# Moving loads, turns, group sums, token turns and cache copies in a two-layer hybrid decoder step on one core

## The chip, the core and the metric

The kernel runs on one core of a Trainium2 chip. A core has five instruction streams that run on their own and meet only at semaphores: TensorE (PE), VectorE (DVE), ScalarE (ACT), GpSimd (POOL) and SyncE (SP, here only a queue that issues transfers). Sixteen DMA engines move data between HBM and SBUF. The metric is the device time of one execution in microseconds (us), lower is better.

## The reference

One inference step of two decoder layers, for a prompt of 256 tokens and 8 decoding sequences of 4 tokens (288 token columns in all), D_MODEL 1024, everything in float32.

```python
def layer(h):
    p = rms_norm(h, norm_w) @ w_in            # q,k,v,gates, indexer, z, x/B/C, dt
    a = sparse_attend(top_k(indexer_scores))  # 4 heads; cache of 2048 rows in pages
    c = dilated_mix(q_c, k_c, v_c)            # 6 heads, windows 128/512/2048, dilation 1/4/16
    y = ssd_branch(z, xbc, dt)                # conv, chunked scan, gated group norm
    return h + concat(a*silu(g_a), c*silu(g_c), y) @ w_out
y = rms_norm(layer(layer(x)), final_norm_w)
```

The group norm divides `y` by the root of the mean square over each of two groups of 192 columns. The outputs are the two streams, the new key and value rows, the states, and the three window caches moved on by four rows; for the caches nearly all bytes are copied unchanged from an input in HBM to an output in HBM.

## The kernel before, in words

Activations lie transposed: 128 features on the partitions, 288 token columns in the free dimension, 8 tiles of features for D_MODEL. A layer is 35 input projection tiles (`proj0` to `proj34`) and 8 output tiles (`out0` to `out7`), each 8 products of a 128x128 weight block with 128x288 columns; the trace shows each product as two matmuls. Between the projections PE does the attention and state products, in an order written out by hand for each engine. Each use of a PSUM bank has a name and a fixed bank in `bank_plan`; `filled(use)` is counted up by PE, `drained(use)` by the engine that reads the bank, and the next use of the same bank waits for `drained` of the last one.

Weights come through four slots (`load_w`, SP queue): the slot of tile i is loaded again, for tile i+4, once tile i is done. Cache pages come through a ring of eight slots `kv`, even items issued by SP and odd ones by POOL, each when PE has used the item eight places earlier. POOL also issues `keep(layer, b, use)`: once `use` is filled, three transfers that copy the window caches of sequence b (2044, 508 and 124 KB) from HBM to HBM. There are 16 of these in all; `FRONT_KEEPS` are issued at the first projections of a layer, `STAGE_KEEPS` from `proj16` to `proj24`, `OUTPUT_KEEPS` behind the last ring item. POOL's last instruction waits for all of them (`copied`).

The stretches that the change touches, in PE's order:

- **Start.** SP loads x (8 tiles) in two transfers, `prm`, then the weights of `proj0`. DVE multiplies x by the norm weight (`weighted`), ACT squares it.
- **Mask and sparse exponential.** PE does two of the eight products of `proj28`, spreads the mask (`msk0` to `msk4`, when DVE's `mask_ready` is up) and does the other six. DVE adds the mask to the scores `srow` and takes the maximum; ACT does `sparse_exp(0..4)`; PE turns each exponentiated quarter (`pt0` to `pt3`); ACT evicts the turns (`sparse_turned`); PE does `value_groups`, 32 groups in all, in portions between the projections. POOL's products `y_gated` stand ahead of both.
- **Group sums and token turns.** ACT squares y (`ysq`); PE sums the squares over the partitions (`gn0`, `gn2`) after `proj30`, then `state_sums(1)`, then turns v of all tokens (`token_rows`: `vc0`, `vc1`, `va0` to `va2`), then `proj31`. DVE works through the last 8 of the `top8_round`s, `state_out(0..7)`, `prompt_mask(1)`, the inverse roots `inverse_group`, `group_normed`, and only then `dilated_scores(0)`.
- **Dilated attention.** `dilated_dots(0)` (PE) -> `dilated_scores(0)` (DVE) -> `dilated_exp(0)` (ACT, behind `evac(32)`) -> `dilated_probs(0)` (DVE) -> `dilated_turn(0)` (PE, after value group 17) -> `dilated_turned(0)` (ACT) -> `dilated_values(0)`; then the same for `qt` = 1.
- **Outputs.** `out0` to `out7`. DVE adds each to x, ACT squares the sum, DVE adds up squares (`add_square`), and PE sums them over the partitions with `sum_squares(L+1, 5)`, which stands between `out6` and `out7`.
- **End.** After the last root, DVE and POOL multiply by it: DVE the tiles 0 to 4 with one instruction each, POOL the tiles 5 to 7, which DVE had multiplied by the weight before. SP issues five transfers of y and waits for them. All engines then drain and meet.

## Time and profile before

| | |
|---|---|
| median of three runs | 609.94 us (609.93 to 610.36) |
| the profiled execution | 606.36 us |
| its span, first to last instruction | 604.6 us |
| busy in it: PE / DVE / POOL / ACT | 555.4 / 354.7 / 241.6 / 175.5 us |
| moved by DMA | 198.37 MB, mean 328 GB/s |
| granted TensorE clock, mean | 0.985 |

The profiled execution ran 1.76 us longer than its span. Idle time of PE is the span less its busy time, 49.2 us; where it lies, and what released PE after it, is what the rows further down are about. In this program the two layers are the same work at about 290 us distance, so a pattern of one stands for both unless said otherwise.

### The profile page before, as it was taken

What the parts mean: (1) busy time and instruction counts of PE and PEld (TensorE: products, weight loads), DVE (VectorE), ACT (ScalarE), POOL (GpSimd) and SP (SyncE); (2) the same over time, 40 slices, a digit from 0 to 9 for tenths busy, and PEclk for the clock granted to TensorE, in tenths of its full rate; (3) what the DMA queues carried; (4) which work ended last, traced back from release to release, by engine and by line L of the source; (5) the groups of instructions that cost most, each with busy time, mean ns of one, the idle gap of its engine ahead of it and who ended that gap; (6) DMA issues with size and microseconds to landing.
All of it is one profiled execution on the core that took longest, in us unless ns stands there. A gap on an engine that the chain in (4) does not pass through costs nothing.

```text
span 604.6 us, 13428 instructions
## 1 busy us (share of the span) xinstructions
PE 555.4 (92%) x4656; PEld 385.6 (64%) x4656; DVE 354.7 (59%) x1081; ACT 175.5 (29%) x457; POOL 241.6 (40%) x433
## 2 busy tenths in 40 slices
PE   4999999999999987999899999999999988799980
PEld 3776655677776654667677565557777755566760
DVE  4864655667776683534267563657678648553223
ACT  3013522112234342641001351311223344264110
POOL 0506642457327446261011474334843464631201
PEclk9999999999999997999999999999999999999996
DMA  8978999999999999798969999999999999993582
GB/s 328 318 279 296 369 368 386 414 355 354 397 395 348 335 307 359 245 347 295 376 208 370 296 362 372 374 417 360 368 367 379 383 336 315 345 322 98 201 302 78
DMA packets 75108, 198.37 MB, mean 328 GB/s; under 512 B 11585, under 2 KB 44770, under 8 KB 70946
## 3 DMA queue, kind: packets, MB, share of 16 engines
q1 hardware_dynamic: 53570, 99.50, 46.7%
q0 software_dynamic: 21472, 98.03, 44.1%
q8 instruction: 37, 0.61, 0.4%
q14 instruction: 29, 0.24, 0.1%
HBM read 189.33 MB, written 52.00 MB: 399 GB/s over the span
## 4 chain that ended last, share of the span: by engine, by line
PE 73%; DMA 9%; DVE 5%; SPq 5%; ACT 5%; issue 2%; DVEq 0%
PE bank L960 69%; DMA kv<-in_kk 6%; SPq L438 4%; PE bank L1006 3%; DMA w<-in_w 3%; ACT shared L765 1%; ACT srow L875 1%; ACT shared L748 1%; DVE shared L1838 1%; DVE shared L1821 1%; DVE st L1827 1%; DVE srow L2174 1%; SPq L434 0%; DVE xn L2256 0%; DVE shared L1785 0%
## 5 line engine op out<-in xcount | busy, mean ns | idle before, releaser
L960 PE MATMUL bank<-xn,w 128*128 128x288 f32 x1120 | 293.8, 416 | 8.2 <-DMA w<-in_w 8.2
L960 PEld LDWEIGHTS bank<-xn,w 128*128 128x128 f32 x1120 | 206.6, 191 | 77.0 <-issue 22.4
L438 POOL DMA_DIRECT2D kv<-in_kk x128 | 68.9, 539 | 91.4 <-PE bank L960 44.2
L438 POOL DMA_DIRECT2D kv<-in_vv x128 | 68.8, 539 | 90.5 <-PE bank L960 49.5
L701 ACT ACTIVATE pt<-bank 128x288 f32<-128x288 f32 x48 | 19.6, 409 | 191.9 <-PE bank L960 191.9
L960 PE MATMUL bank<-pt,w 128*128 128x288 f32 x256 | 64.1, 408 | 1.2 <-DMA w<-in_w 1.2
L960 PEld LDWEIGHTS bank<-pt,w 128*128 128x128 f32 x256 | 48.1, 190 | 15.4 <-DMA w<-in_w 2.0
L541 POOL DMA_DIRECT2D out_keep<-in_buf x48 | 25.0, 527 | 81.1 <-PE bank L960 79.3
L1696 DVE TENSOR_SCALAR_CACHE_REDUCE hit<-sc,tb 128x516 bf16<-128x516 f32 x62 | 46.5, 750 | 2.2
L960 PE MATMUL bank<-kv,qz 128*32 128x256 f32 x512 | 34.3, 385 | 0.0
L960 PE MATMUL bank<-kv,pt 128*32 128x256 f32 x512 | 33.5, 391 | 0.0
L2242 DVE TENSOR_TENSOR x<-x,bank 128x288 f32<-128x288 f32 x16 | 7.3, 454 | 40.0 <-PE bank L960 40.0
L1669 DVE COPY tails<-cin 128x3 f32<-128x3 f32 x14 | 4.8, 344 | 44.1 <-ACT cin L699 41.9
L960 PE MATMUL bank<-pt 64*128 64x128 f32 (+3 forms) x168 | 27.5, 351 | 0.0
L670 ACT ACTIVATE phased<-x 128x288 f32<-128x288 f32 x24 | 10.4, 442 | 58.5 <-DVE x L2242 52.7
L960 PEld LDWEIGHTS bank<-pt 64*128 64x128 f32 (+2 forms) x168 | 18.7, 193 | 11.6 <-issue 10.6
L1675 DVE SCALAR_TENSOR_TENSOR cacc<-cin,prm,cacc 128x312 f32<-128x312 f32 x42 | 22.8, 544 | 1.5
L1707 DVE TENSOR_SCALAR tb<-bank 128x1 int32<-128x1 f32 x62 | 9.6, 155 | 23.8 <-PE bank L960 23.1
L431 POOL DMA_DIRECT2D kv<-in_dil x16 | 8.7, 547 | 35.5 <-PE bank L960 35.3
L960 PEld LDWEIGHTS bank<-kv,pt 128*32 128x32 f32 x512 | 14.4, 111 | 12.1 <-issue 4.7
L960 PEld LDWEIGHTS bank<-kv,qz 128*32 128x32 f32 x512 | 13.4, 109 | 11.8 <-issue 6.3
L960 PE MATMUL bank<-kv,shared 128*32 128x128 f32 x576 | 18.6, 275 | 0.0
(262 smaller groups left out, 737.6 us busy)
## 6 DMA issues: line engine op xcount, KB each, us to landing
w<-in_w SPq DMA_DIRECT2D x86, 512.0 KB, 8.6
out_keep<-in_buf POOLq DMA_DIRECT2D x16, 2044.0 KB, 13.9
kv<-in_kk SPq DMA_DIRECT2D x128, 160.0 KB, 8.4
kv<-in_kk POOLq DMA_DIRECT2D x128, 160.0 KB, 5.8
kv<-in_vv SPq DMA_DIRECT2D x128, 128.0 KB, 4.8
kv<-in_vv POOLq DMA_DIRECT2D x128, 128.0 KB, 4.8
kv<-in_dil SPq DMA_DIRECT2D x16, 576.0 KB, 11.4
kv<-in_dil POOLq DMA_DIRECT2D x16, 576.0 KB, 8.1
```

Source lines behind the costliest of these rows:

```text
L431: engine.dma_start(kv[:, s, 0:9 * P], a["dil"][layer, item // NB * NB + SEQ_ORDER[item % NB]]).then_inc(S[f"kv_in{s}"], 16)
L438: engine.dma_start(kv[:, s, r * rec:(r + 1) * rec], a["kk" if what == "page" else "vv"][bass.ds(page + layer * N_POOL, 1)].rearrange("o p ...
L541: pool.dma_start(a[f"keep{g}"][bass.ds(layer, 1), b], a[f"buf{g}"][bass.ds(layer, 1), b, 4 * 256:], max_dma_last_dim=COPY_ROW).then_inc(S[ ...
L670: act.activation(squares[:, k % 2, 0:T], x[:, k, :], ACT.Square).then_inc(S["sq_ready"], 1)
L701: act.activation(ptile(i), src[:, 0:T], fn).then_inc(use, 1)
L748: act.activation(psa[:, i, 0:nk], psa[:, i, 0:nk], ACT.Exp, bias=st8[:, 1, i:i + 1], accum_out=st8[:, 2, i:i + 1]).then_inc(S["pexp"] if i ...
L960: return pe.matmul(out, lhsT, rhs, start=start, stop=stop, skip_group_check=True, **k)
L1006: return pe.transpose(out, in_, ident(n))
L1675: stt(out=o, in0=cin[:, n % 2, j:j + COUT], scalar=prmc(L, "cw", 4 * n + j), in1=o, op0=ALU.mult, op1=ALU.add).then_inc(S["cin_used"] if j ...
L1696: ts_(hit[:, :], sc[:, :], old.bitcast(F32), 0.0, ALU.is_ge, ALU.add, accum_out=cnt[:, 0:1]).then_inc(S["cnt_ready"], 1)
L1707: ts_(tb[:, 2:3], src[:, 0:1], float(TOPK_S), float(bit), ALU.is_lt, ALU.mult).then_inc(drained(f"count{n}"), 1)
L2242: tt_(x[:, m, :], x[:, m, :], src[:, 0:T], ALU.add).then_inc(drained(f"out{m}"), 1)
```

## The change

It reorders and moves; no arithmetic is removed.

- **Loads at the start.** x comes in four transfers of two tiles. SP issues `prm`, tiles 0-1, the weights of `proj0`, tiles 4-5; ACT issues tiles 2-3 and 6-7 as its first instructions.
- **Mask.** PE does one product of `proj28` ahead of the mask in place of two.
- **Turns.** ACT does the five `sparse_exp` in a row; DVE evicts `pt0` and `pt1` in place of ACT, and the `top8_round` that stood there moves behind.
- **Group sums.** ACT squares y ahead of `evac(28)`, loads the root's table with a small instruction, and takes the roots between `evac(29)` and `evac(30)`. PE does `gn0` between `state_sums(0)` and value group 6, `gn2` ahead of `proj30`. The banks of `gn2`, `ss4` to `ss7`, `vc1`, `va0` change.
- **Token turns.** From before `proj31` to after `proj32`.
- **Dilated exponential.** ACT does it ahead of `evac(32)`; DVE does `dilated_scores(0)` ahead of the second inverse and of `group_normed`, and `dilated_probs(0)` right after the second inverse.
- **Square sums.** `sum_squares(L+1, 5)` moves into `out7`, after five of its eight products.
- **Copies.** Each stage issues four in place of five; the second layer's end issues four in place of two, two of them at `proj34`. The front of layer 1 has two as before.
- **End.** DVE does all eight tiles, POOL none. SP issues two transfers of y, ACT two.

```diff
-FRONT_KEEPS = ((), ((0, 7, "proj1"), (1, 0, "proj4")))
-STAGE_KEEPS = (((0, 0), (0, 1), (0, 2), (0, 3), (0, 4)), ((1, 1), (1, 2), (1, 3), (1, 4), (1, 5)))
-OUTPUT_KEEPS = (((0, 5, "out0"), (0, 6, "out4")), ((1, 6, "out0"), (1, 7, "out2")))
+FRONT_KEEPS = ((), ((0, 6, "proj1"), (0, 7, "proj4")))
+STAGE_KEEPS = (((0, 0), (0, 1), (0, 2), (0, 3)), ((1, 0), (1, 1), (1, 2), (1, 3)))
+OUTPUT_KEEPS = (((0, 4, "out0"), (0, 5, "out4")), ((1, 4, "proj34"), (1, 5, "proj34"), (1, 6, "out0"), (1, 7, "out1")))
...
-                       ("gn0", 3), ("gn2", 2), ("ss4", 5), ("ss5", 6), ("ss6", 7), ("ss7", 3),
-                       ("vc0", 2), ("vc1", 5), ("va0", 2), ("va1", 6), ("va2", 5),
+                       ("gn0", 3), ("gn2", 3), ("ss4", 2), ("ss5", 5), ("ss6", 6), ("ss7", 7),
                        ("dot", 7), ("pd00a", 3), ("pd01a", 5), ("pd00b", 6), ("pd01b", 2),
+                       ("vc0", 2), ("vc1", 3), ("va0", 5), ("va1", 6), ("va2", 2),
...
-            for n in range(2):
-                sync.dma_start(x[:, 4 * n:4 * n + 4, :], a["x"][:, 4 * n:4 * n + 4, :]).then_inc(S[f"x_in{n}"], 16)
             sync.dma_start(prm[:, :, :], a["prm"]).then_inc(S["prm_in"], 16)
+            sync.dma_start(x[:, 0:2, :], a["x"][:, 0:2, :]).then_inc(S["x_in0"], 16)
             load_w(0, 0)
+            sync.dma_start(x[:, 4:6, :], a["x"][:, 4:6, :]).then_inc(S["x_in2"], 16)
...
-            for name, n, lo, hi in (("y_normed", 2, 0, 2), ("y_normed", 4, 2, 4), ("y_pooled", 2, 6, 8), ("y_normed", 5, 4, 5), ("y_pooled", 3, 5, 6)):
-                sync.wait_ge(S[name], n)
-                sync.dma_start(a["y"][:, lo:hi, :], xn[:, lo:hi, :]).then_inc(S["y_out"], 16)
-            sync.wait_ge(S["y_out"], 80)
+            for n in (0, 2):
+                sync.wait_ge(S["y_normed"], 2 * n + 2)
+                sync.dma_start(a["y"][:, 2 * n:2 * n + 2, :], xn[:, 2 * n:2 * n + 2, :]).then_inc(S["y_out"], 16)
+            sync.wait_ge(S["y_out"], 64)
...
                 feat(KC, KC + 3, 5)
-                keep(*STAGE_KEEPS[L][4], "proj24")
...
-            pool.wait_ge(S["rstd_ready"], nth(DEPTH, "rstd_ready", 1))
-            for k in (6, 7, 5):
-                pool.wait_ge(S["xw_ready"], nth(DEPTH, "xw_ready", k - 4))
-                pool.tensor_tensor(xn[:, k, :], xn[:, k, :], rstd[:, :], ALU.mult).then_inc(S["y_pooled"], 1)
...
         def _(act):
+            for n in (1, 3):
+                act.dma_start(x[:, 2 * n:2 * n + 2, :], a["x"][:, 2 * n:2 * n + 2, :]).then_inc(S[f"x_in{n}"], 16)
...
-                sparse_exp(0)
-                sparse_exp(1)
-                sparse_turned(0)
-                sparse_exp(2)
-                sparse_turned(1)
-                sparse_exp(3)
-                sparse_exp(4)
+                for c in range(5):
+                    sparse_exp(c)
                 sparse_turned(2)
                 sparse_turned(3)
...
-                evac(28)
-                evac(29)
-                evac(30)
                 for t in range(3):
                     act.wait_ge(S["y_ready"], nth(L, "y_ready", t + 1))
                     act.activation(xwf[:, t * T:(t + 1) * T], ptile(ZZ + t), ACT.Square).then_inc(S["ysq"], 1)
-                act.wait_ge(filled("gn2"), nth(L, "gn2"))
+                evac(28)
+                act.activation(warm[:, :], eps[:, :], ACT.Sqrt).then_inc(chain.next(), 1)
+                evac(29)
                 for t in (0, 2):
+                    act.wait_ge(filled(f"gn{t}"), nth(L, f"gn{t}"))
...
+                evac(30)
+                evac(31)
+                dilated_exp(0)
+                evac(32)
                 tokens("vc", 0, 256, 640)
                 tokens("vc", 1, 256, 640)
                 for tt in range(3):
                     tokens("va", tt, 0, 256)
-                evac(31)
-                evac(32)
-                dilated_exp(0)
                 dilated_turned(0)
...
-                proj(28, 0, 2)
+                proj(28, 0, 1)
                 pe.wait_ge(S["mask_ready"], nth(L, "mask_ready", 1))
...
-                proj(28, 2)
+                proj(28, 1)
...
                 proj(29)
...
                 state_sums(0)
+                group_sums(0, ((0, slice(0, P)), (1, half(0))))
                 value_groups(6, 9)
+                group_sums(2, ((1, half(1)), (2, slice(0, P))))
                 proj(30)
                 state_sums(1)
                 value_groups(9, 12)
-                pe.wait_ge(drained(f"y{2}"), nth(L, "y2"))
-                token_rows("vc", 0, VC, 3)
-                token_rows("vc", 1, VC, 3)
...
                 proj(32)
+                pe.wait_ge(drained(f"y{2}"), nth(L, "y2"))
+                token_rows("vc", 0, VC, 3)
+                token_rows("vc", 1, VC, 3)
...
-                for m in range(2, KT):
-                    output(m, (0, 1) if m == 2 else (5, 6, 7, 2, 3, 4, 0, 1))
-                    if m == KT - 2:
-                        pe.wait_ge(drained("pat11"), nth(L, "pat11"))
-                        sum_squares(L + 1, KT - 3)
+                output(2, (0, 1))
+                for m in range(3, KT - 1):
+                    output(m, (5, 6, 7, 2, 3, 4, 0, 1))
+                output(KT - 1, (5, 6, 7, 2, 3))
+                pe.wait_ge(drained("pat11"), nth(L, "pat11"))
+                sum_squares(L + 1, KT - 3)
+                output(KT - 1, (4, 0, 1))
...
-                top8_round(1)
+                dve.wait_ge(S["ki_out"], nth(L, "ki_out", 16))
+                dve.wait_ge(S["y_ready"], nth(L, "y_ready", 3))
+                for jg in range(2):
+                    dve.wait_ge(filled(f"pt{jg}"), nth(L, f"pt{jg}"))
+                    dve.tensor_copy(sct[:, 4 * jg:4 * jg + 4, :].rearrange("p j n -> p (j n)"), bank_of(f"pt{jg}")[:, :]).then_inc(drained(f"pt{jg}"), 1)
                 dve.wait_ge(S["sexp"], nth(L, "sexp", 5))
...
-                for n in range(4):
+                for n in range(6):
                     top8_round(1)
                 for b in range(4):
                     state_out(b)
                 prompt_state_out()
-                for n in range(3):
+                for n in range(2):
                     top8_round(1)
+                inverse_group(0)
                 for b in range(4, NB):
                     state_out(b)
                 prompt_mask(1)
-                inverse_group(0)
+                dilated_scores(0)
                 inverse_group(2)
+                dilated_probs(0)
                 group_normed()
-                dilated_scores(0)
...
-            for k in range(5):
+            for k in range(KT):
                 dve.scalar_tensor_tensor(out=xn[:, k, :], in0=x[:, k, :], scalar=fnw[:, k:k + 1], in1=rstd[:, :],
                                          op0=ALU.mult, op1=ALU.mult).then_inc(S["y_normed"], 1)
```

With it go the names of the semaphores (`x_in0` to `x_in3`; `y_pooled` is gone), the wait of each square and product of the start for its own quarter of x, and two y transfers at the end of ACT's program.

## Rows read from the trace of the kernel before

**Rows 1.** Waits of PE from 20 to 600 us: us in total, times, longest.

```profile
PE bank L1006 <- DVE shared L1838: 7.8, 4, 3.2
PE bank L1006 <- ACT srow L875: 3.9, 6, 0.7
...
PE bank L960 <- ACT xw L924: 3.0, 2, 1.5
PE bank L960 <- DVE phased L1622: 2.8, 2, 1.4
PE bank L960 <- ACT xw L927: 1.4, 2, 0.7
PE bank L960 <- DMA w<-in_w: 1.2, 1, 1.2
```

**Rows 2.** Timeline around the sparse exponential, layer 1: start us, us, instruction.

```profile
484.46 0.72 ACT L875 ACTIVATE srow<-srow,st 128x512 f32<-128x512 f32 x1 [1.86 <-DVE st L2182]
...
486.02 0.60 ACT L881 ACTIVATE pt<-bank 128x512 f32<-128x512 f32 x1
...
489.35 0.85 PE L960 MATMUL bank<-kv,pt 128*32 128x256 f32 x12
```

**Rows 3.** Groups by shape: count, busy us, mean ns, idle before.

```profile
L1918 DVE COPY sc<-bank 128x512 f32<-128x512 f32 x2 | 1.4, 690 | 5.6 <-PE bank L960 5.6
...
L1994 DVE TENSOR_TENSOR phased<-phased,bank 128x384 f32<-128x384 f32 x16 | 8.9, 554 | 0.6
...
L2009 DVE RECIPROCAL xw<-xw 128x288 f32<-128x288 f32 x4 | 7.8, 1953 | 0.1
...
L1733 DVE MAX8 top<-iacc 128x8 f32<-128x256 f32 x16 | 6.8, 428 | 0.6
...
L701 ACT ACT_TABLE_LOAD x8 | 10.3, 1283 | 0.1
```

**Rows 4.** Timeline of PE: dilated turns, layer 1's start, group sums.

```profile
235.68 1.54 PE L1006 MATMUL bank<-const,shared 128*128 128x128 f32 x6 [3.23 <-DVE shared L1838]
...
248.91 1.53 PE L1006 MATMUL bank<-const,shared 128*128 128x128 f32 x12 [0.58 <-DVE shared L1838]
...
301.81 4.04 PE L960 MATMUL bank<-xn,w 128*128 128x288 f32 x16
...
504.09 2.12 PE L960 MATMUL bank<-xw,ones 128*128 128x288 f32 x8 [1.49 <-ACT xw L924]
...
526.50 0.87 PE L1006 MATMUL bank<-const,shared 128*128 128x128 f32 x6 [3.23 <-DVE shared L1838]
...
537.19 1.53 PE L1006 MATMUL bank<-const,shared 128*128 128x128 f32 x12 [0.81 <-DVE shared L1838]
```

**Rows 5.** Windows: busy us of each engine, granted PE clock, DMA share, GB/s.

```profile
235.00:240.00 5.00, 4.32 (x26) 2.58 (x28) 0.63 (x2) 1.15 (x3) 2.15 (x4) 0.50 1.04 374
...
555.00:560.00 5.00, 4.58 (x25) 3.21 (x25) 2.81 (x4) 2.57 (x4) 0.00 (x0) 1.00 0.00 0
...
570.00:575.00 5.00, 5.00 (x22) 3.90 (x22) 0.95 (x3) 0.44 (x1) 0.00 (x0) 1.00 1.02 408
```

**Rows 6.** The chain that ended last, at the start: start us, us, what.

```profile
2.26 5.83 DMA w<-in_w
```

**Rows 7.** Weights issued at 286.57 us, copy issued at 568.35 us: us to landing.

```profile
w<-in_w SPq DMA_DIRECT2D x1, 512.0 KB, 14.5
...
out_keep<-in_buf POOLq DMA_DIRECT2D x1, 2044.0 KB, 20.0
```

**Rows 8.** GpSimd's last instructions: duration ns min/median/max, first and last start.

```profile
L226 POOLq DRAIN  x1: 10912/10912/10912, 593.5 to 593.5; - x1
```

**Rows 9.** VectorE's y products and GpSimd's, as in rows 8.

```profile
L2256 DVE SCALAR_TENSOR_TENSOR xn<-x,fnw,rstd x5: 503/1037/1046, 593.0 to 596.3; 128x288 f32<-128x288 f32 x5
...
L654 POOL TENSOR_TENSOR xn<-xn,rstd x3: 940/995/999, 593.2 to 595.1; 128x288 f32<-128x288 f32 x3
```

**Rows 10.** The y transfers, time from issue to landing.

```profile
DMA to landing us min/median/max: 2.1/2.3/2.5
```

More of the change, by code:

```diff
@@ L209 @@
 PER = {
-    "rstd_ready": 1, "sq_ready": 8, "sq_used": 5, "y_normed": 5, "y_pooled": 3, "z_gated": 1, "xw_ready": 8, "xn_free": 7, "xn_ready": 8, "roped": 15, "shuffled": 7, "ssum_ready": 1, "root_ready": 1,
+    "rstd_ready": 1, "sq_ready": 8, "sq_used": 5, "y_normed": 8, "z_gated": 1, "xw_ready": 8, "xn_free": 7, "xn_ready": 8, "roped": 15, "shuffled": 7, "ssum_ready": 1, "root_ready": 1,
     "qs_ready": 1, "relu_used": 1, "prelu_used": 8, "cnt_ready": NCOUNT + 1, "cin_used": 7, "tanhed": 7, "conved": 7,
@@ L331, in build @@
         S = {name: ctx.enter_context(nc.semaphore(name))
-             for name in ("x_in0", "x_in1", "ptab_in", "prm_in", "cst_in", "const_in", "ones_set", "zeroed", "act_chain", "dve_chain", "pool_chain", "y_out",
+             for name in (*[f"x_in{n}" for n in range(4)], "ptab_in", "prm_in", "cst_in", "const_in", "ones_set", "zeroed", "act_chain", "dve_chain", "pool_chain", "y_out",
                           *[f"w_in{n}" for n in range(WSLOTS)], *[f"kv_in{n}" for n in range(NKV)], *PER)}
@@ L664, in square @@
                 if N == 0:
-                    act.wait_ge(S[f"x_in{k // 4}"], 16)
+                    act.wait_ge(S[f"x_in{k // 2}"], 16)
                 else:
@@ L952, in _ @@
                 act.sem_clear(S["act_chain"])
+            for n in (1, 3):
+                act.wait_ge(S["y_normed"], 2 * n + 2)
+                act.dma_start(a["y"][:, 2 * n:2 * n + 2, :], xn[:, 2 * n:2 * n + 2, :]).then_inc(S["y_out"], 16)
         @block.tensor
@@ L1508, in _, with group_sums @@
                 proj(29)
-                state_sums(0)
-                value_groups(6, 9)
-                proj(30)
-                pe.wait_ge(S["ysq"], nth(L, "ysq", 3))
-                for t, parts in ((0, ((0, slice(0, P)), (1, half(0)))), (2, ((1, half(1)), (2, slice(0, P))))):
+                def group_sums(t, parts):
+                    pe.wait_ge(S["ysq"], nth(L, "ysq", 3))
                     pe.wait_ge(drained(f"gn{t}"), before(L, f"gn{t}"))
@@ L1518, in _ @@
                     ins.then_inc(filled(f"gn{t}"), 1)
+                state_sums(0)
+                group_sums(0, ((0, slice(0, P)), (1, half(0))))
+                value_groups(6, 9)
+                group_sums(2, ((1, half(1)), (2, slice(0, P))))
+                proj(30)
                 state_sums(1)
                 value_groups(9, 12)
-                pe.wait_ge(drained(f"y{2}"), nth(L, "y2"))
-                token_rows("vc", 0, VC, 3)
-                token_rows("vc", 1, VC, 3)
-                pe.wait_ge(drained(f"proj{VA + 1}"), nth(L, f"proj{VA + 1}"))
-                for tt in range(3):
-                    token_rows("va", tt, VA, 2)
                 proj(31)
@@ L1535, in _ @@
                 proj(32)
+                pe.wait_ge(drained(f"y{2}"), nth(L, "y2"))
+                token_rows("vc", 0, VC, 3)
+                token_rows("vc", 1, VC, 3)
+                pe.wait_ge(drained(f"proj{VA + 1}"), nth(L, f"proj{VA + 1}"))
+                for tt in range(3):
+                    token_rows("va", tt, VA, 2)
                 value_groups(16, 18)
@@ L1849, in _ @@
                     for k in range(KT):
-                        if k % 4 == 0:
-                            dve.wait_ge(S[f"x_in{k // 4}"], 16)
+                        if k % 2 == 0:
+                            dve.wait_ge(S[f"x_in{k // 2}"], 16)
                         weighted(0, k)
@@ L2212, in _ @@
                     tt_(gate, src[half(h2), 0:384].rearrange("p (g c n) -> p g c n", g=3, c=4)[:, :, :, h2:16:2], gate, ALU.mult).then_inc(drained("dot") if h2 else chain.next(), 1)
-                dilated_probs(0)
                 dilated_scores(1)
@@ L2245, in _ @@
                         weighted(L + 1, m)
-                    elif m >= 5:
-                        dve.wait_ge(drained(f"out{m}"), nth(L, f"out{m}"))
-                        ts_(xn[:, m, :], x[:, m, :], fnw[:, m:m + 1], None, ALU.mult).then_inc(S["xw_ready"], 1)
                     if 1 < m < KT - 1:
```

## The prediction

> **What bounds the kernel now.** I read the page first. PE is busy 555.4 of 604.6 us, and where the DMA engines work they are full, with a share of 1.02 to 1.04 [rows 5], so the question is who waits for whom. The waits of PE answer it [rows 1]: between 20 and 600 us PE waits for a weight transfer once, 1.2 us in all, and otherwise for VectorE and ScalarE in the stretch after the mask: 7.8 us for the dilated probabilities (four times, two of them 3.2 us), 3.9 for the sparse exponentials, 3.0 and 1.4 around the group sums, 2.8 for the square sums at a layer's end. PE's order sets the time, and what can be won is its idle time: these waits, the 8 us before its first matmul, and what lies behind its last. The timeline of PE [rows 4] shows where each wait lies; the windows [rows 5] show that the wait in layer 0 has a second price, a halved clock; the last rows [rows 8] show that the span ends with an instruction of GpSimd, not with the y transfers.
>
> **The start.** PE's first matmul follows the landing of `proj0`'s weights, issued at 2.26 us and 5.83 us on the way [rows 6]. Ahead of and with them went all of x, `prm` and the weights: 1152 + 51 + 512 = 1715 KB. Now tiles 4-5 (288 KB) are behind them; the tiles issued by ACT share the engines with them. At the 408 GB/s that a full window shows [rows 5], 288 KB are 0.7 us. If ACT's 576 KB took nothing from them, it would be 864 KB and 2.1 us; if the landing is set by something other than bytes, nothing. I take **-0.7**. DVE needs `prm` and tiles 0-1, which are now first; tiles 6-7 are wanted last.
>
> **Mask and exponentials, per layer.** PE spreads the mask right behind two products of `proj28`; the first exponential began at 484.46 and the value groups at 489.35 [rows 2]. One product is two matmuls, and a full window of 5 us holds 22 [rows 5]: 0.47 us sooner for mask, maxima and exponentials (nothing, if `mask_ready` is what comes last). The two evictions between the exponentials, 0.60 us each with 0.1 overlap, leave the chain: 486.02 was 1.56 behind 484.46 for two exponentials, so four now take 3.1 us, and 1.0 us is saved. DVE's copies of a 128x512 bank cost 0.69 each [rows 3]; they lie beside the third and fourth exponential, ahead of `px_ready`, which waits for the fifth anyway. If they did not hide, 0.7 of the 1.0 would be gone. PE waited 3.9/2 here in a layer, so 1.95 is the most. I take **-1.5**.
>
> **Group sums, per layer.** ScalarE squared behind `evac(30)`, and PE waited 1.5 us for the squares and 0.7 for the roots [rows 1, 4]. The squares now come ahead of `evac(28)`, two projections before PE wants them, and PE has three value groups or `proj30` to do while each root is taken: **-2.2**, at least 1.5 (the squares alone).
>
> **Dilated turns, per layer.** DVE did `inverse_group` twice (1.95 us each [rows 3]), `group_normed` and ScalarE `evac(32)` ahead of the first dilated softmax; PE waited 3.23 us for it in each layer [rows 4]. Now the scores come before the second inverse, which lies under the exponential; and the turns of v (1.5 us of PE) come after `proj32`, between scores and turn. The softmax is ready by my count 3 us before PE comes: **-3.2**. The second wait (0.6 and 0.8 us) stays, since the distance from `dilated_dots(1)` to it is what it was.
>
> **What is late next, per layer.** `dot` now takes bank 7 from `ss7`, which DVE drains last. DVE's queue from `state_sums(0)` on: `state_out(0..3)` 8 x 0.55 = 4.4, the prompt's state 2 x 0.55 = 1.1, two rounds of a MAX8 at 0.43, a replacement of the same size and small ones, 2.2, the first inverse 1.95, `state_out(4..7)` 4.4, together 14.1 us [rows 3]. PE does in that time the two group sums (8 matmuls, 2.0), `proj30` and `proj31` (16 each, 3.9), six value groups and `state_sums(1)` (64 small ones, 3.6): 13.4. PE waits **+0.7** for it (0 to 2: the sum of so many terms is no better). Behind it on PE stand the dilated dots. POOL's long wait for `ss7` only moves along. ScalarE gets one more table load in a layer, 1.28 us [rows 3], between two exponentials or while it waits for `proj32`: nothing, as the wait there is longer.
>
> The Trainium skill (ScalarE: Activation LUTs, What ACT_TABLE_LOAD costs) counts 2.66 us for a switch with its drain, where the row has 1.28. By that an eviction of v would be about 0.5 us late for `va2` in each layer, and the sum 1 us smaller.
>
> Per layer -1.5 - 2.2 - 3.2 + 0.7 = -6.2, for two **-12.4**.
>
> **The clock.** In layer 0 the wait of 3.23 us was followed by a window at a granted 0.50 [rows 5], that is 1.2 in place of 2.4 GHz. From the first dilated turn to the second PE took 248.91 - 235.68 = 13.2 us there, and 537.19 - 526.50 = 10.7 in layer 1, where the same wait left the clock alone [rows 4]. With the wait gone, **-2.5** (0 if another gap does it, the longest left there being 0.8 us).
>
> **Layer ends.** PE waited 1.4 us for the squares between `out6` and `out7` [rows 1]; five products (2.4 us) now cover it. In layer 1 that is -1.4. In layer 0 the weights of the next `proj0`, issued at 286.57, landed 14.5 us later, at 301.1 [rows 7], and that projection began at 301.8 [rows 4]. It can't begin before: **-0.7**, as the engines are full there.
>
> **Copies.** One copy (2044 + 508 + 124 KB) leaves each stage. No wait of PE in the stage was for a transfer, so I give nothing for it; it makes room for the same pages in less time. The end has four: two go out at `proj34`, when the engines stand idle (0 GB/s at 555 to 560 us [rows 5]). 5.35 MB at 408 GB/s are 13 us, which end before `out0` sends the other two and the last weights. The timeline has `proj34`'s end at 547 and `out0`'s at 565; no term of the sum comes from these two. They cost nothing there, and if they ran on past `out0`, the last copy would land later, which the end has room for (below).
>
> **The end.** DVE began y at 593.0. Of its five products those beside POOL's took 1037 ns, the one without 503 [rows 9]. PE's 1.4 us puts the start at 591.6; eight at 0.5 end at 595.6; ScalarE issues the last transfer, 2.5 us to land [rows 10]: 598.2. But the span ended with GpSimd's DRAIN, begun at 593.5 and 10.9 long, until 604.4 [rows 8], while the last product of y was begun at 596.3 [rows 9] and a transfer takes 2.5 [rows 10]. POOL's work now ends with the last copy, 568.35 + 20.0 = 588.4 [rows 7]. If the drain is 10.9 us long from there, it ends at 599.3; if it is 8.3 us behind POOL's last work (595.1 + 1.0 before [rows 9]), at 596.7. So the end lies between 598.2 and 599.5; I take 599.0, **-5.6** with layer 1's 1.4 in it.
>
> The rule against this part is in the Trainium skill (SBUF — State Buffer, Who interferes with whom): a VectorE instruction with two SBUF inputs and a GpSimd instruction that reads SBUF exclude each other. The trace agrees, 1037 against 503 ns, and it speaks for the change, since POOL has no product left. Without the rule eight products at 1.0 us would end at 599.9 and y land at 602.4, and the sum would be 3.4 us smaller.
>
> **Sum.** -0.7 - 12.4 - 2.5 - 0.7 - 5.6 = -21.9 us. On the profiled execution that is 606.36 - 21.9 = 584.5. The median of the runs shown is 3.6 us above it, which no row explains; I carry it along: 609.94 - 21.9 = **588.0 us**.
>
> **Rivals.**
> - *The drain does not move with POOL's work*, but ends as far behind everything as before. For it: the row shows one drain only, with nothing to compare. Then the end gives 1.4 in place of 5.6: 592.2 us. 15%.
> - *Transfers take the place of the waits.* A window in the stage has a DMA share of 1.04 at 374 GB/s [rows 5]: full. If the ring can't deliver in 6 us less, the stages return up to 12.4: 600.4 us, half of it 594.2. Against it: PE waited for no page there, and a copy of 2.7 MB less frees 7.2 us at that rate. 10%.
> - *The runs without a profile lose the clock in layer 1 as well*, which would explain most of the 3.6 us. Then 2.5 more come back: 585.5 us. 13%.
> - *The other side: the four copies end last.* POOL waits for them and drains after it. The rest is 16.3 us earlier, so the kernel is slower only if the last copy lands after about 610 on the old scale in place of 588.4, that is if the 10.7 MB of copies and 2.6 of weights from 549 on move at under 215 GB/s, where full windows show 374 and 408. At 200 GB/s: 614 us. 2%.
> - *It does nothing*, if each wait is replaced by the next one: 610 us. 2%.
> - The forecast, 583 to 592 by its own terms: 55%. The last 3% are losses that I don't see, between 595 and 609.
>
> The range from 583 to 595 takes in the clock rival, the drain rival and half the transfer rival. A change of 0.2%, 1.2 us, is about what a measurement of this kernel can tell from none. Faster by more 96%, within 1.5%, slower 2.5%.
>
> **What would show it.** PE's first matmul at 7.4 us; waits of PE for L1838 down from 7.8 to about 1.5 us, for the two ScalarE lines of the group sums gone, for the exponentials under 2; a new wait of 0.7 us for DVE's `state_out`, twice; no window at 0.50 inside; no wait between `out6` and `out7`; a DRAIN of POOL that begins at the last copy's landing and ends by 583 us. Wrong I would be with waits for `kv` or `w` in the stages, or a drain that still ends last by 4 us.

## The result

The changed kernel takes **586.82 us** (median of four runs, 584.74 to 590.63) against 609.93 for the kernel before (four runs): ratio 0.9636, 95% interval 0.9602 to 0.967, 23.1 us less. The forecast was 588.0 with a range of 583 to 595. The profiled execution took 584.74 us with a span of 583.1; the sum had put it at 584.5. It was the fastest of the four, 2.1 us under their median, where the kernel before had 3.6 us between the two.

The waits of PE from 15 us to the end (us in total, times, longest), to be held against [rows 1]:

```profile
PE bank L956 <- DMA kv<-in_vv: 4.5, 3, 2.1
PE bank L956 <- DMA kv<-in_kk: 2.9, 3, 1.1
PE bank L956 <- DMA w<-in_w: 1.3, 4, 0.5
PE bank L956 <- ACT relun L782: 1.1, 2, 0.6
PE bank L1002 <- DVE shared L1802: 0.8, 2, 0.4
PE bank L956 <- ACT phased L667: 0.5, 1, 0.5
PE bank L1002 <- ACT srow L872: 0.5, 2, 0.2
```

All the lines at which the change aimed are gone or small: the dilated probabilities (7.8 us), the two ScalarE lines of the group sums (3.0 and 1.4), the square sums (2.8); the exponentials are down from 3.9 to 0.5. In their place stand transfers: 4.5 us for value pages (`in_vv`), a line that the kernel before does not have, and four short waits for weights. [Rows 1] leave out this line of the kernel before:

```profile
PE bank L960 <- DMA kv<-in_kk: 3.4, 6, 0.9
```

These six waits for key pages, at 80 to 104 and at 370 to 395 us, lie ahead of the mask and are 2.9 us now.

The timeline of PE shows where the value pages are waited for. Start, duration, instruction, and in brackets the idle time before it:

```profile
195.95 3.11 PE L956 MATMUL bank<-kv,pt 128*32 128x256 f32 x48
...
227.79 0.87 PE L1002 MATMUL bank<-const,shared 128*128 128x128 f32 x6
228.59 1.07 PE L956 MATMUL bank<-kv,pt 128*32 128x256 f32 x16
229.59 1.57 PE L956 MATMUL bank<-pt 64*128 64x256 f32 x12
231.09 0.88 PE L956 MATMUL bank<-shared,vtok 128*64 128x128 f32 x12
234.05 1.08 PE L956 MATMUL bank<-kv,pt 128*32 128x256 f32 x8 [2.09 <-DMA kv<-in_vv]
235.06 5.28 PE L956 MATMUL bank<-xn,w 128*128 128x288 f32 x16
...
241.33 0.88 PE L1002 MATMUL bank<-const,shared 128*128 128x128 f32 x6
...
291.95 4.12 PE L956 MATMUL bank<-xn,w 128*128 128x288 f32 x16
...
509.03 0.87 PE L1002 MATMUL bank<-const,shared 128*128 128x128 f32 x6
...
515.22 0.64 PE L956 MATMUL bank<-kv,pt 128*32 128x256 f32 x8 [2.01 <-DMA kv<-in_vv]
...
520.92 1.53 PE L1002 MATMUL bank<-const,shared 128*128 128x128 f32 x12
```

The first dilated turn (227.79, 509.03) has no wait before it; one value group later, at group 20, PE stands still for 2.09 and 2.01 us until its page lands. `proj33` behind it takes 5.28 us in layer 0, where an undisturbed projection takes 4.15: part of it ran at half the clock. The windows (busy us of each engine, granted clock, DMA share, GB/s) say the same, and one thing more:

```profile
175.00:180.00 5.00, 5.00 (x43) 3.88 (x41) 3.99 (x14) 1.64 (x8) 0.00 (x0) 1.00 0.72 270
180.00:185.00 5.00, 5.00 (x86) 3.97 (x86) 2.43 (x9) 0.00 (x0) 1.47 (x3) 1.00 0.19 56
...
230.00:235.00 5.00, 2.91 (x32) 1.52 (x28) 3.96 (x8) 0.50 (x1) 3.72 (x8) 0.90 1.05 374
235.00:240.00 5.00, 5.00 (x20) 3.73 (x16) 1.84 (x5) 3.23 (x5) 0.48 (x1) 0.76 1.05 365
```

The clock of 235 to 240 us was 0.50 before [rows 5] and is 0.76 now. And the DMA engines, full from 190 to 245 us, are almost idle at 180 to 185, where the fifth copy of the stage used to be.

The end, in GpSimd's last instructions and VectorE's y products (ns min/median/max, first and last start; as [rows 8, 9]):

```profile
L226 POOLq COMPARE_BRANCH  x1: 41/41/41, 573.7 to 573.7; - x1
L226 POOLq DRAIN  x1: 8487/8487/8487, 573.9 to 573.9; - x1
...
L2259 DVE SCALAR_TENSOR_TENSOR xn<-x,fnw,rstd x8: 514/514/519, 577.0 to 580.0; 128x288 f32<-128x288 f32 x8
```

Eight products at 514 ns, no longer 1037, one every 0.43 us. The DRAIN is over at 582.38, the last y transfer lands at about 582.7, and the span ends at 583.1.

**Where the 21.5 us of span went.** From landmark to landmark on PE, change against the kernel before:

| stretch | forecast | measured |
|---|---|---|
| to the first matmul | -0.7 | -1.26 |
| to the value groups, layer 0; from the mask on, layer 1 | -1.5 each | -1.32, -1.18 |
| to the first dilated turn | -4.7 each | -5.31, -5.05 |
| to the second dilated turn | -2.5 (clock), 0 | +0.31, +1.20 |
| to `proj0` of layer 1 | -0.7 | -2.28 |
| to layer 1's mask (nothing edited) | 0 | -1.38 |
| to layer 1's last square sums | -1.4 | +0.21 |
| to the end | -4.2 | -5.44 |

### The profile page after: what moved, and what is told of

It reads as the page before. It is cut to its first block, busy times and chain, and to the rows that moved or that the text cites. A ratio compares the mean times of both kernels' runs of the same rounds, so it can differ in the third digit from the quotient of the medians.

```text
span 583.1 us, 13433 instructions
## 1 busy us (share of the span) xinstructions
PE 555.4 (95%) x4656; PEld 385.4 (66%) x4656; DVE 355.3 (61%) x1085; ACT 176.2 (30%) x457; POOL 238.7 (41%) x430
## 3 DMA queue, kind: packets, MB, share of 16 engines
q10 hardware_dynamic: 576, 1.18, 0.6%
## 4 chain that ended last, share of the span: by engine, by line
PE 73%; DMA 17%; SPq 3%; DVE 2%; issue 2%; ACT 2%; POOL 1%; POOLq 0%; DVEq 0%; ACTq 0%
PE bank L956 71%; DMA kv<-in_kk 7%; DMA kv<-in_vv 5%; DMA w<-in_w 5%; SPq L438 2%; PE bank L1002 2%; ACT shared L745 1%; DVE xn L2259 1%; DVE shared L1787 0%; DVE shared L1802 0%; DVE st L1792 0%; POOL kv L438 0%; DVE rstd L1615 0%; ACT pt L899 0%; SPq L434 0%
## 5 line engine op out<-in xcount | busy, mean ns | idle before, releaser
L698 ACT ACTIVATE pt<-bank 128x288 f32<-128x288 f32 x48 | 19.7, 410 | 180.3 <-PE bank L956 180.3
L956 PE MATMUL bank<-pt 64*128 64x128 f32 (+3 forms) x168 | 26.3, 334 | 0.0
L1709 DVE TENSOR_SCALAR tb<-bank 128x1 int32<-128x1 f32 x62 | 9.6, 155 | 23.8 <-PE bank L956 23.1
L956 PEld LDWEIGHTS bank<-kv,qz 128*32 128x32 f32 x512 | 13.4, 109 | 11.8 <-issue 6.3
## 6 DMA issues: line engine op xcount, KB each, us to landing
out_keep<-in_buf POOLq DMA_DIRECT2D x16, 2044.0 KB, 13.9
```

The source lines that it names most:

```text
L698: act.activation(ptile(i), src[:, 0:T], fn).then_inc(use, 1)
L956: return pe.matmul(out, lhsT, rhs, start=start, stop=stop, skip_group_check=True, **k)
L1709: ts_(tb[:, 2:3], src[:, 0:1], float(TOPK_S), float(bit), ALU.is_lt, ALU.mult).then_inc(drained(f"count{n}"), 1)
```

## The experiments

Each ran in rounds beside the kernel before on the same chip; the ratio is to that kernel. Its own median was 608.9, 609.4 and 608.0 us in the three sets (e1 to e4, e5 to e7, e8 to e10) over 11 to 15 runs. The sets ran on three chips, so experiments of different sets are compared by ratio: 0.001 is 0.6 us.

**e1, the start and the end alone**, on the kernel before: the diff's parts for the loads of x, the y products and the y transfers.

> The kernel before with two parts of the change alone: the loads at the start and the end (all eight y products on VectorE, two y transfers each from SP and ScalarE, none on GpSimd). Copies and everything between stay as before. Theory: the two parts are worth what the trace of the changed kernel shows at its two ends, first matmul at 6.9 us in place of 8.2 (-1.3) and 8.7 us in place of 14.0 from PE's last matmul to the end (-5.3): 609.9 - 6.6 = 603.3 us, GpSimd's DRAIN over before the y transfers land. Rival: the end's gain comes from the copies that land earlier in the changed kernel; here they land as before, GpSimd's DRAIN then ends last again, and the whole gives -1.3 to -3: 607 to 608.6 us.

Measured: 603.44 us, ratio 0.9898 (0.9864 to 0.9932). The first matmul started at 6.92 us, and PE's waits in between are those of before. The two ends are worth 5 to 6 us in the time, nearly what the theory said, without any help from the copies' new places. By landmarks they save 6.7 us (1.3 to the first matmul, 5.4 behind the last square sums), and 1.3 us in between are lost, where this profile has two windows at a clock of 0.66 in layer 1 that the kernel before does not have.

```profile
L226 POOLq DRAIN  x1: 8242/8242/8242, 589.9 to 589.9; - x1
```

The last copy landed at 589.6 here, the DRAIN behind it took 8.24 us and was over about 0.7 us before the y transfers.

**e2, the copies as before**, on the changed kernel:

```diff
-STAGE_KEEPS = (((0, 0), (0, 1), (0, 2), (0, 3)), ((1, 0), (1, 1), (1, 2), (1, 3)))
-OUTPUT_KEEPS = (((0, 4, "out0"), (0, 5, "out4")), ((1, 4, "proj34"), (1, 5, "proj34"), (1, 6, "out0"), (1, 7, "out1")))
+STAGE_KEEPS = (((0, 0), (0, 1), (0, 2), (0, 3), (0, 4)), ((1, 1), (1, 2), (1, 3), (1, 4), (1, 5)))
+OUTPUT_KEEPS = (((0, 5, "out0"), (0, 6, "out4")), ((1, 6, "out0"), (1, 7, "out2")))
+                keep(*STAGE_KEEPS[L][4], "proj24")
```

> The changed kernel with the copies placed as before: five in each stage (the fifth at proj24), two in each stretch of outputs. Theory: the engines are nearly idle at 180 to 185 us in the changed kernel (0.19), just where the fifth copy stood, and full from 190 on, so the copy is out of the way before the value pages are late. The waits of PE for value pages stay at about 2 us in each layer (4.1 to 4.9 us in all), the waits for weights in layer 1's outputs (1.3 us) go, and the time is 0.5 to 1.5 us under the changed kernel's 586.8: 585.3 to 586.3. Rival: the copy less is what paid for the pages that are now wanted sooner; then 2.7 MB more at 360 GB/s make PE's waits for pages grow by several us in each layer, and the time is 592 to 600 us.

Measured: 585.22 us (583.94 without its longest run), ratio 0.9598 (0.9538 to 0.9659), not to be told from the changed kernel. PE's waits for value pages are 5.3 us in place of 4.5, those for weights 2.4 in place of 1.3. The engines' share at 180 to 185 us is 0.96 again, no longer 0.19. So the rival is out: a copy more in the stage does not bring 592 to 600 us. But half of the theory is out as well: the weights of layer 1's last outputs come just in time here too. Two copies issued with them at `out0` to `out2` are enough for that; the two at `proj34` are not needed for it.

**e3, the late group behind the projection**, on the changed kernel:

```diff
-                value_groups(20, 21)
                 proj(33)
+                value_groups(20, 21)
```

(and SP's list of `next_w` follows: `(12, 18), (18, 20), (20, 26)`)

> The changed kernel with value group 20, the one that waited 2.1 us for its page in each layer, behind proj33 in place of ahead of it; nothing else moves. Theory: the page lands at its time whatever PE does, the engines being full up to it, and proj33 (4.1 us) covers it. The two waits of 2.0 us go; the second wait for the dilated softmax comes back (0.6 and 0.8 us before), and the window of layer 0 at half clock, which followed the wait (1.7 us of cost), goes or stays. So -2.6 without and -4.3 with the clock: 582.5 to 584.2 us. Rival: supply is behind by bytes, and the next groups (21 to 25) wait in its place: 586.3 to 587.3 us, with page waits of 4 us as before.

Measured: 581.4 us, ratio 0.9541 (0.9499 to 0.9583); again as e10: 582.27, 0.9574 (0.954 to 0.9608). From the first to the second dilated turn PE takes 10.68 us in layer 0 and 10.69 in layer 1, where the changed kernel takes 13.54 and 11.89. The waits at group 20 are gone, the second wait for the dilated softmax is back (1.6 us for both), and no window below full clock is left while PE works. The page itself is as late as before (issued from 221.3 us, landed at 234.7): `proj33` covers it. Of the rival, 0.87 us of waiting for a later page in layer 0 is left.

**e4, the dilated exponential's part undone**, on the changed kernel:

```diff
-                dilated_scores(0)
                 inverse_group(2)
-                dilated_probs(0)
                 group_normed()
+                dilated_scores(0)
+                dilated_probs(0)
...
-                dilated_exp(0)
                 evac(32)
+                dilated_exp(0)
```

> The changed kernel with the dilated exponential's part undone: VectorE does the scores behind the second inverse and group_normed, ScalarE the exponential behind evac(32). Theory: the pages set the floor of this stretch. PE waits 1 to 3 us for the first dilated turn again in each layer, but the wait for the page of value group 20 falls by the same, so that of up to 2 us in each layer nothing shows in the time: 586.8 to 589 us. Rival: the page wait is no floor but comes at its own place whatever precedes it (the order of the issues behind it sets it); then the waits add up, and the time is 589 to 593 us.

Measured: 589.22 us, ratio 0.9651 (0.9607 to 0.9694), by the medians 2 to 3 us over the changed kernel, where theory and rival meet; the intervals overlap, so the times do not decide. The waits of PE in the profile:

```profile
PE bank L1002 <- ACT vtok L738: 4.8, 2, 2.4
...
PE bank L956 <- DMA kv<-in_vv: 0.4, 1, 0.4
```

4.8 us of a new wait (ScalarE evicts the token turns only behind the exponential), and 4.1 us less for pages. In layer 0 the page landed at 233.7 us, 13.1 us after its issue, with the changed kernel at 234.0. The second dilated turn came at 240.95 us, with the changed kernel at 241.33: the page was the floor, and a first turn 2.5 us later cost nothing. In layer 1 the turn was late by 2.9 us counted from the mask, 1.5 us of it in a stretch at half clock. So in layer 0 the page took back what the dilated part of the change had gained; in layer 1 about half of it shows.

**e5, the changed kernel again.**

> The changed kernel once more, as the yardstick on this chip for the two beside it. Theory: 0.9636 of before again, and within a kernel the slower runs are those with the lower mean granted clock, since the windows at half clock come and go between runs. Rival: time and mean clock of the runs have nothing to do with each other.

Measured: 586.47 us, ratio 0.9613 (0.9572 to 0.9654). In this profile the page of group 20 cost 3.80 us in layer 0 and 2.14 in layer 1. Time and clock go together, but not closely: the kernel before took 604.6 us at a mean granted clock of 0.988 and 612.2 at 0.981 (the ends of ten of its eleven runs), the changed one 584.87 at 0.996 and 590.65 at 0.988 (of six). In e10 the fastest and the slowest of five runs, 5.0 us apart, had 0.994 and 0.995, so part of the spread is not the clock's.

**e6, layer 1's last copies late, SP waits for them**, on the changed kernel: `(1, 6, "out4"), (1, 7, "out5")`, and `wait_ge(S["copied"], ...)` moved from GpSimd's end to SP's.

> The changed kernel with two edits at its end: the last two copies of layer 1 go out at out4 and out5 in place of out0 and out1, and SP in place of GpSimd waits for all copies. Theory: in layer 1 the weights of out4 to out7 landed 5.7 to 13.2 us after their issue because two copies stood on the engines with them; without those they land in 5 to 8 us, PE's waits for weights in layer 1's outputs (about 1.3 us, with the weight loads' own 2.6) go, and PE ends 1.5 to 2.5 us sooner. GpSimd's DRAIN, 8.2 to 8.5 us long wherever it begins, now begins near 560 us and ends by 570; the last copy (20 us from issue at 560 at most) lands before y: 584.5 to 585.5 us. Rival: the weights queue behind what was issued earlier (the copies of proj34), and nothing changes; or the last copy ends last: 587 to 590 us.

Measured: 585.84 us, ratio 0.962 (0.9572 to 0.9668): no difference that shows. At PE the theory holds: no output of layer 1 waits for weights, and it gets from the turn ahead of the outputs (544.65 us in the changed kernel) to the last square sums in 27.1 us, the changed kernel in 28.9. The end gives it back:

```profile
L226 POOLq DRAIN  x1: 19153/19153/19153, 562.8 to 562.8; - x1
...
L226 SPq DRAIN  x1: 7/7/7, 580.8 to 580.8; - x1
```

The DRAIN begins at 562.8 as wanted and lasts 19.15 us, until 581.97: 4.3 us behind the last copy's landing at 577.7. The theory had it 8.2 to 8.5 us long wherever it begins; that step is refuted.

**e7, the copies spread**, on e3: two at the front of layer 0 (`proj4`, `proj6`), five in each stage, one at `proj34` in each layer, none in the outputs.

> Value group 20 behind proj33 as in e3, and the copies where the trace of the changed kernel has room: two in the front of layer 0 (proj4, proj6), the fifth one back at proj24 in each stage (the engines were at a share of 0.19 there), one at proj34 in each layer and none in the outputs; SP waits for all copies. Theory: e3's 581.4, less the weight waits of both layers' outputs (3 us at PE in e3: 1.5 in each layer) and of the first projection of layer 1: 577.5 to 580 us, page waits of the stages as in e3. Rival: copies in the front of layer 0 delay its weights or first pages, and give back what the outputs gain: 581 to 583 us.

Measured: 593.52 us, ratio 0.9729 (0.9683 to 0.9775), 12 us over e3. By ratio it is 9 to 11 us. The rival had the direction; its size was some four times too small. The timeline of PE:

```profile
52.05 7.08 PE L957 MATMUL bank<-xn,w 128*128 128x288 f32 x16 [5.56 <-DMA w<-in_w]
...
284.01 11.27 PE L957 MATMUL bank<-pt,w 128*128 128x288 f32 x33 [4.25 <-DMA w<-in_w]
```

The weights of `proj8` were issued 0.3 us ahead of the first copy and needed 22.2 us, where the three tiles ahead of them had needed 5 to 9. The engines were full there before the copy came (a share of 1.02 at 25 to 30 us), with key pages on the way. The layer 0 copy of `proj34` went out 5 us ahead of the weights of `out4`, which needed 10.0 us; the one of layer 1 caused no wait. After both waits the clock fell:

```profile
50.00:55.00 5.00, 2.95 (x6) 2.17 (x7) 0.00 (x0) 0.00 (x0) 0.54 (x1) 0.62 0.98 355
...
285.00:290.00 5.00, 5.00 (x12) 3.43 (x11) 0.00 (x0) 0.00 (x0) 0.00 (x0) 0.50 0.17 69
```

Twelve matmuls in five busy microseconds, where a window at full clock has 22.

**What makes that page late.** The chain of the changed kernel at group 20, and GpSimd's issues beside it:

```profile
220.69 0.33 SPq L438
...
224.19 9.82 DMA kv<-in_vv
234.01 0.04 issue
234.05 7.34 PE bank L956 x28
```

```profile
217.18 2.29 POOL L438 DMA_DIRECT2D kv<-in_vv  x4 [0.41 <-issue]
219.46 0.54 POOL L639 DMA_DIRECT2D out_s_ssd<-phased  x1
220.00 0.54 POOL L640 DMA_DIRECT2D out_p_ssd<-xws  x1
222.44 2.33 POOL L438 DMA_DIRECT2D kv<-in_vv  x4 [1.90 <-PE bank L956]
```

SP issues the page's four pieces from 220.69 on, and the last lands at 234.01, 13.3 us later. 1.2 us ahead of it GpSimd has sent the states, 1536 and 192 KB, as soon as `ss7` is drained. Before, the two issues were these:

```profile
223.57 0.54 POOL L640 DMA_DIRECT2D out_s_ssd<-phased  x1
...
227.20 9.13 SPq L438 DMA_DIRECT2D kv<-in_vv  x11
```

The store had 3.6 us of lead on the page, which landed in 9.4 us, and PE wanted it 15.4 us after its issue; now PE is at group 20 11.3 us after it.

**e8, the store behind the pages**, on the changed kernel:

```diff
+                consumed(*RING[60:64])
                 pool.wait_ge(drained(f"ss{NB - 1}"), nth(L, f"ss{NB - 1}"))
                 pool.dma_start(a["s_ssd"][ly]...)
                 pool.dma_start(a["p_ssd"][ly]...)
-                consumed(*RING[60:64])
```

> The changed kernel with one edit: GpSimd issues the two stores of the states (1536 and 192 KB) behind the value pages of groups 21 and 23 in place of ahead of them, in both layers. Theory: in the changed kernel the store goes out at 219.46 us and the page of group 20 from 220.69 us on; the page lands 13.3 us after its issue, at 234.0, and PE waits 2.1 us for it, where in the kernel before the store had 3.6 us of lead (223.57, 227.20) and the page landed after 9.4 us. 1728 KB are 4.7 us at 370 GB/s. With the store behind the page, the page lands by 230, the page waits of about 2 us (3.8 in the repeated run) go in both layers, the second wait for the dilated softmax (0.6 and 0.8 us) comes back, and the half clock behind the wait goes in most runs: 581.5 to 584 us against 586.5. Rival: the bytes have only changed places, and the pages of groups 21 to 25 come late by the same amount: 586 to 588 us.

Measured: 584.0 us, ratio 0.9597 (0.9565 to 0.9628), and five runs within 1.3 us, where the changed kernel's six in e5 were 5.8 apart. By ratio that is 1.0 to 2.4 us under the changed kernel, and the intervals overlap: what e8 shows is the page, not yet a gain in time. The timeline of PE in layer 0:

```profile
230.93 0.88 PE L956 MATMUL bank<-shared,vtok 128*64 128x128 f32 x12
231.74 0.64 PE L956 MATMUL bank<-kv,pt 128*32 128x256 f32 x8
232.31 4.15 PE L956 MATMUL bank<-xn,w 128*128 128x288 f32 x16
236.38 1.12 PE L956 MATMUL bank<-vtok,cin 32*128 32x256 f32 x4
238.32 1.53 PE L1002 MATMUL bank<-const,shared 128*128 128x128 f32 x12 [0.81 <-DVE shared L1840]
```

Group 20 without a wait, `proj33` in 4.15 us, the second softmax's 0.81 back. The page landed 5.9 us after its issue in place of 13.3, and in layer 1 group 20 has no wait either. The pages of 24 to 27 now take 10 to 12 us and are wanted late enough. What keeps the whole time up in this profile lies elsewhere, ahead of the moved stores: in layer 1 the exponentials were waited for 1.41 us (0.25 in the changed kernel), and group 5 for its page 1.92 us (0.38 there).

```profile
480.60 0.64 PE L956 MATMUL bank<-kv,pt 128*32 128x256 f32 x8 [1.92 <-DMA kv<-in_vv]
```

No run tells whether that belongs to e8 or to this one execution.

**e9, e8 with the copies of e2** and layer 1's last two at `out3` and `out4`, SP waiting for them.

> The store moved as in e8, the copies of the kernel before but for the last two (five in each stage, layer 1's last two at out3 and out4), SP waiting for all copies at the end. Theory: e8, and the weights of layer 1's out4 to out7 no longer land beside copies: 1.5 to 2 us less at PE there; GpSimd's DRAIN ends about 4.2 us behind the last copy's landing (as in e6), with that landing near 572: 579.5 to 582.5 us. Rival: the DRAIN or y transfers beside the last copy give it back at the end: as e8.

Measured: 581.98 us, ratio 0.9565 (0.953 to 0.96). PE waits 0.4 us for weights in all. The last copy landed at 577.1, not 572, and the DRAIN took 19.7 us until 581.1, about 4 us behind that landing and 1.5 us ahead of the span's end, so that y decided.

**e10, e3 again.**

> e3 once more, beside e8 and e9 on the same chip. Theory: 581 to 582 us again; the gain over the changed kernel (586.5) is real and not a matter of the chip. Rival: it was luck of the runs' clocks, and it comes out at 584 to 587 us.

Measured: 582.27 us, ratio 0.9574, as said at e3; 0.3 us over the range of its theory. e3 and e9 are the best versions and not to be told apart. By ratio they are 2.4 to 5.8 us under the changed kernel. The intervals of e3 and e9 lie below the changed kernel's first (0.9602 to 0.967), that of e10 touches it, and all three overlap that of e5 (0.9572 to 0.9654) at its edge. A gain is likely, and its size is open.

## Why the forecast was right, and where its steps were not

The median is 1.2 us under the forecast, and the sum of the steps (-21.9) is the change of the span (-21.5). The dilated softmax, the group sums, the exponentials and the end, which make up most of the sum, came as reasoned. But the sum also holds errors of up to 2.8 us in a stretch: 5.6 us were missed between the dilated turns and in layer 1's outputs, and 5.2 us came on top elsewhere. That they cancel to 0.4 us is luck; the experiments show where most of them come from.

- **The start (-0.7, measured -1.26).** The chain has the weights issued at 1.79 us, no longer at 2.26, and 5.04 us on the way in place of 5.83. The time on the way fell by 0.79, which fits the 0.7 worked out from the bytes; that one issue less stands ahead of them gave 0.47, a term that was not in the sum. Among the profiles with these loads the first matmul starts between 6.84 and 7.77 us (e5), so single values are good to half a microsecond.
- **Mask and exponentials (-1.5 each; -1.32, -1.18).** Right.
- **Group sums and dilated turns (-5.4 each, less 0.7 for `dot`; -5.31, -5.05).** Right, but for the wait at `dot`: from 204 us on VectorE took 13.9 us to the end of `state_out(7)` (14.1 counted), PE 14.3 to its start at 218.25 (13.4 counted; the group sums took 2.9 and not 2.0), so the wait is 0. The first softmax was ready at 225.1 (VectorE's last product, 224.24 + 0.87) for a turn at 227.79, 2.7 us of slack where 3 were counted. The added table load stands in the wait for `proj29`; no eviction of v came late for it, so neither 1.28 nor the 2.66 us of the Trainium skill (ScalarE: Activation LUTs, What ACT_TABLE_LOAD costs) shows in the sum. The load's 1.28 us began as the instruction ahead of it ended, at 197.97, and the next one started 0.02 us behind it.
- **"The second wait stays, since the distance is what it was", and the clock's -2.5: the step that failed.** Both supposed that nothing else is late between the two dilated turns. The page of group 20 was: +2.09 and +2.01 us in place of the second wait's 0.58 and 0.81. In layer 0 this new gap stands just where the old one did, and the half clock (1.2 GHz) stayed for 3.4 us, where it had been 6.9 (from the windows: 0.10 + 0.24 of 5 us below full clock now, 0.03 + 0.50 + 0.16 before, each doubled). Without these two waits PE took 11.45 us between the turns, where it had taken 12.65, so 1.2 us of the clock's -2.5 came; the longer gap took 1.5: +0.31. e8 takes the gap away, and the stretch takes 10.7 us at full clock (2.4 GHz), as the forecast had it.
- **The rival "transfers take the place of the waits" had the right place and the wrong cause.** It argued from bytes over the whole stage, and the argument against it (a copy less frees 7.2 us) was as wrong: at 180 to 185 us the engines now stand nearly idle, and no queue issues a page from 164 to 182 us, the ring being full, so that the pages can't use the room that the fifth copy leaves; with the copy back in it (e2) the time is the same. What counts here is what goes out just ahead of one page: e8 moves the stores of the states and nothing else, and the page is in time. The forecast's list of what PE waits for left out the key pages (3.4 us), so "PE waited for no page" holds only from the mask on. There it was true, but it did not show how little there was to spare: 15.4 us from issue to use, with 9.4 needed.
- **Layer 0's end (-0.7, measured -2.28).** The limit was the one named, the landing of the next `proj0`'s weights (landed 291.88, first used 291.95). But that landing was no constant: 12.9 us on the way, 14.5 before [rows 7]. The extra 1.6 us are that; why it was shorter no run isolates.
- **Layer 1's end (-1.4, measured +0.21).** VectorE's wait is gone, and the weights of `out4` to `out7` land 0.04 us before their use, 5.7, 8.9, 12.6 and 13.2 us after their issue. "They cost nothing there" was said of the two copies at `proj34`, and e2 bears it out; the other two, issued along with the weights, hold them up (e6: 1.9 us come back at PE when they go out later).
- **The end (-4.2, measured -5.44).** The forecast chose 599.0 of 598.2 to 599.5. y was ready sooner (a product each 0.43 us, not 0.5; a landing in 2.1 to 2.2 us), and the DRAIN behind the last copy took 8.49 us, not 10.9, near the 8.3 of the reading that the forecast weighed and did not take. e1 has the same end without the rest of the change: 9.5 us from the last square sums to the end of the span, with the changed kernel 9.5, before 15.0. That VectorE's products take 514 ns with GpSimd silent, and 1037 beside it [rows 9], agrees with the rule of the Trainium skill (SBUF — State Buffer, Who interferes with whom). The rival that the drain does not move with GpSimd's work is out.
- **Layer 1's front, where nothing was edited (-1.38).** The same stretch took 177.9 to 179.5 us in this profile, in that of before and in eight of the experiments' (181.4 and 181.7 in e4 and e9, which had a window at 0.66 in it), so this is the spread of single executions.
- **The 3.6 us between the profiled execution and the median**, carried along unexplained, and 2.1 us for the changed kernel: those 1.5 us less put the median under the forecast, since the profiled execution lies 0.2 us over the sum. The runs' granted clocks explain some of it: the profiled execution of before had 0.985, and its sixteen runs from 609 to 614.9 us beside e1 to e10 had 0.978 to 0.985, fourteen of them 0.982 or less. At 0.5 us for each 0.001, the slope through the 36 runs, 0.003 would be 1.5 us; the rest stays open. e1's profile has windows at 0.66 in layer 1, at 485 and 525 us, which the profile of before does not have. So the rival "runs without a profile lose the clock in layer 1 as well" describes something real: a profiled execution can have it or not.

## What to carry to other kernels

A wait that is removed brings PE to the next transfer sooner: for each transfer behind it, read issue, landing and use, and ask whether the slack covers the time won; a list of waits that names no transfer in a stretch only says that the slack was not negative. When a transfer becomes late, look first at what another queue issues in the microseconds ahead of it: here moving one large store behind the page brought it in time, which one copy fewer in the stage had not done. And put bulk copies where the engines are idle and no weights are on the way: a copy at `proj24` cost nothing that shows (e2), three moved to `proj4`, `proj6` and layer 0's `proj34` 9 to 12 us (e7).

## What was not expected of the hardware

- GpSimd's DRAIN at the end was 8.2 to 8.5 us long when its transfers had landed before it began (the changed kernel, e1 to e5, e8, e10); begun earlier, it lasted until 3.9 to 4.3 us behind the landing of the last of its copies (14.2 us in e7, 19.2 in e6, 19.7 in e9). In those three SP waited for the copies, and the DRAIN still outlasted them.
- A 512 KB weight transfer took 3.4 to 5.2 us with the engines free. Issued beside a 2.7 MB copy or up to 4 us behind it, it took 5.7 to 13.2 us in the changed kernel's outputs, and 18.5 to 22.2 us in e7, where key pages were on the way as well. Issued 0.2 us ahead of a copy, with only other weights on the engines, it took 3.8 us (e9, issued at 556.1 us): the copy alone does not make the 22.
- A stretch at half clock followed gaps of very different length. The shortest is in e4, in a part that no edit touched: the window from 425 to 430 us has a clock of 0.66 with PE busy all through, and a gap of 1.04 us stands ahead of it.

```profile
424.48 0.50 PE L956 MATMUL bank<-ad,const 6*128 6x288 f32 x1 [1.04 <-issue]
424.92 2.78 PE L956 MATMUL bank<-xn,w 128*128 128x288 f32 x6
```

After the gap between the dilated turns it came in some profiles (the changed kernel 2.09 us, e5 3.80 and 2.14, layer 1 of e1 3.22 ahead of the first turn) and not in others (e2 2.80, e6 2.18, layer 1 of the kernel before 3.23). What decides between the two stays open.
